# FFN of a two-layer encoder step: up projection as seven block products on sums of x halves, plain down products woven between

## The chip, the core and the metric

The kernel runs on one NeuronCore of a Trainium2 chip. Five engines work at once, each through its own list of instructions in order, and wait for one another through semaphores: PE (TensorE, matrix products), DVE (VectorE), ACT (ScalarE), POOL (GpSimd) and SP, which here only issues DMAs. The metric is the device time of one execution in microseconds (us); lower is better.

## What is computed

Two layers, each on 576 tokens (64 of running streams, 512 of new ones). A layer is a mixer (GLA and RWKV-7 groups between an input and an output projection), and a convolutional feed-forward network (FFN), each added to `x`. Only the FFN is touched:

```python
def _conv_ffn(h, conv_prev, w_up, conv_w, conv_b, w_down):   # h = RMSNorm(x), D = 1024, F = 2816
    uv = jnp.einsum('bld,df->blf', h, w_up)                  # 1024 -> 2 * 2816
    u, gate = uv[..., :D_FF], uv[..., D_FF:]
    u_ext = jnp.concatenate([conv_prev.astype(u.dtype), u], axis=1)
    uc = conv_b + sum(conv_w[j] * u_ext[:, j:j + seq] for j in range(CONV_W))
    conv_new = u_ext[:, seq:]
    y = jnp.einsum('blf,fd->bld', jax.nn.gelu(uc, approximate=False) * gate, w_down)   # 2816 -> 1024
    return y, conv_new
```

## The kernel before

**Layout.** Activations lie transposed: 128 features on the partitions, the 576 tokens along the row, so `x` is eight tiles of 128 x 576. An output tile of a product is one row of blocks; it is made in two halves of 288 tokens (`HT`), each in a PSUM bank of its own.

**Precision.** Every fp32 product is made of three passes in the rounded type fp32r: weights and activations are split into a high part (`whi`, `xh`, `hh`, `Hhi`: a rounded copy, made by ACT) and a low part (`wlo`, `xl`, `hl`, `Hlo`: original less high part, made by POOL for the weights as loaded, and by DVE for activations and for sums of weights). The passes are high x high, high x low, low x high. So an output tile over `n` inner tiles costs PE 6n matmuls of 288 columns.

**Pairs.** Work runs in pairs of output tiles: slot 0 and slot 1 have their own raw weights (`raw`, 128 x 1024, one DMA of 512 KB), their `whi`/`wlo` and, in a plain pair, PSUM tensors `PS[0]` and `PS[1]`. For each slot: SP loads `raw` once POOL's last low part there is made (`load`, L453), ACT rounds (`split`, L1436), POOL subtracts (`split` of POOL, L635), PE multiplies (`dense`, L790), DVE reads PSUM.

**The FFN before** goes in three parts of 8, 8 and 6 inner tiles (`PARTS`). There are 22 up pairs, all plain: slot 0 gives `u`, slot 1 the gate of one inner tile, 2 x 8 x 6 = 96 matmuls. For each, DVE scales `u` by the norm (`nrs`) into `up` (L2669 to L2671), keeps the last two columns (L2675), does two of the three convolution taps (L2680, L2683; ACT the first, L1960), scales the gate (L2690), and after ACT's GELU (L1967) multiplies (L2693, L2695); ACT and DVE then make high and low parts of the inner tile. In the first two parts DVE also forms four sums of halves of inner tiles (`T1` to `T4`). The down products of these two parts (4 pairs each) are *folded*: a 2 x 2 block product made of seven block products instead of eight (Strassen-Winograd form). Its weights are four quarters `A11, A12, A21, A22`; DVE makes the sums `S1` to `S4` (L2603, 128 x 512 each) and their low parts (L2608), ACT the high parts (L1910), POOL the low parts of `A11, A12, A22` (L731). A folded pair is 7 x 4 x 3 = 84 matmuls (L1335 to L1337). It uses four banks, and the pairs take the two sets of four banks in turn (`quad_banks`). The third part's four down pairs are plain with 6 inner tiles. At a part's border one up pair is issued ahead of the folded pairs, so that its DVE work lies beside them.

**Order.** It is written out by hand for each engine. PE waits in `product` for the low part of its quarter (`d_rest`, `w_lo`, `d_lo`), for ACT's copies between banks (`d_copy`), and before the last product for a DVE add (`d_add`).

## Time and profile before

| | us |
|---|---|
| median of 3 runs (1603.68 to 1604.71) | 1604.25 |
| the profiled execution: its time | 1609.08 |
| the profiled execution: its span | 1607.1 |
| PE busy, DVE busy, ACT busy, POOL busy in it | 1571.3, 1101.5, 707.8, 601.8 |

The profile is of one execution; it is read by engine, by stretch and by single rows. Busy time of DVE and POOL holds also the time in which an instruction has begun and is held up, so that a long row is not always long work. The FFN of layer 0 runs from about 390 to 808 us, that of layer 1 from about 1180 to 1594 us.

### The profile page before, as it was taken

The page shows a single profiled execution, that of the slowest core. Times are in us where ns is not written, and L with a number is a line of the kernel's source. Part 1 is how long each engine was busy: PE and PEld are TensorE (multiplying, and loading weights), DVE is VectorE, ACT ScalarE, POOL GpSimd, SP SyncE. Part 2 cuts the span into 40 slices and gives each one's busy share as a digit, 9 for nine tenths or more (in the row PEclk, how much of TensorE's full clock was granted, in tenths as well). Part 3 has the DMA queues.
Part 4 walks back from the last instruction along what each step waited for, and adds up shares of the span by engine and source line. Part 5 has one row for each costly group of instructions (what it writes and reads, how often), then busy time and mean ns, then how long its engine had stood idle before and what let it go on. Part 6 is the DMA issues. An engine that isn't in the chain of part 4 may idle for free.

```text
span 1607.1 us, 40959 instructions
## 1 busy us (share of the span) xinstructions
PE 1571.3 (98%) x17831; PEld 1530.0 (95%) x17831; DVE 1101.5 (69%) x1747; ACT 707.8 (44%) x1174; POOL 601.8 (37%) x394
## 2 busy tenths in 40 slices
PE   8999999999999999999999999999999999999997
PEld 7999989899999999999999999888999999999997
DVE  4679656675778677856647894566667786787664
ACT  5545356553334333433454644556433343334334
POOL 5345422223344343434333453122234434343331
PEclk9999999999999999999999999999999999999999
DMA  5222210012322322232332222000223232323222
GB/s 157 66 80 79 66 43 4 4 35 83 88 80 73 99 80 88 83 94 74 89 96 74 72 79 74 10 4 4 60 80 90 81 92 80 92 66 105 83 73 90
DMA packets 219123, 115.42 MB, mean 72 GB/s; under 512 B 9588, under 2 KB 216706, under 8 KB 218946
## 3 DMA queue, kind: packets, MB, share of 16 engines
q1 hardware_dynamic: 218866, 112.79, 24.7%
q8 instruction: 141, 2.31, 0.6%
q14 instruction: 36, 0.29, 0.1%
q10 hardware_dynamic: 80, 0.02, 0.0%
HBM read 109.27 MB, written 3.53 MB: 70 GB/s over the span
## 4 chain that ended last, share of the span: by engine, by line
PE 89%; DVE 5%; issue 2%; DMA 2%; POOL 1%; ACT 1%; SPq 0%; DVEq 0%; ACTq 0%
PE ps L758 31%; PE ps L759 31%; PE ps L1335 3%; PE ps L1337 3%; PE ps L1336 3%; PE ps L1008 2%; PE ps L1011 2%; PE ps L1005 2%; DMA raw<-in_ffn_w_down 1%; DVE Tall L2603 1%; PE ps L970 1%; POOL wlo L731 1%; PE ps L982 1%; PE ps L1073 1%; PE ps L763 1%
## 5 line engine op out<-in xcount | busy, mean ns | idle before, releaser
L635 POOL TENSOR_TENSOR wlo<-raw,whi 128x1024 fp32r<-128x1024 f32 (+1 forms) x169 | 432.3, 2558 | 621.2 <-ACT whi L1436 621.2
L1436 ACT ACTIVATE whi<-raw 128x1024 fp32r<-128x1024 f32 (+1 forms) x170 | 176.6, 1039 | 384.1 <-PE ps L759 359.4
L758 PE MATMUL ps<-xh,whi 128*128 128x288 f32 x1120 | 331.7, 296 | 1.8 <-DVE xl L2017 1.8
L759 PE MATMUL ps<-xh,whi 128*128 128x288 f32 x1120 | 329.4, 294 | 0.0
L758 PE MATMUL ps<-xl,whi 128*128 128x288 f32 x1120 | 329.3, 294 | 0.0
L759 PE MATMUL ps<-xl,whi 128*128 128x288 f32 x1120 | 329.3, 294 | 0.0
L758 PE MATMUL ps<-xh,wlo 128*128 128x288 f32 x1120 | 329.1, 294 | 0.0
L759 PE MATMUL ps<-xh,wlo 128*128 128x288 f32 x1120 | 328.8, 294 | 0.0
L758 PEld LDWEIGHTS ps<-xh,whi 128*128 128x128 f32 x1120 | 210.2, 188 | 3.8 <-issue 3.1
L759 PEld LDWEIGHTS ps<-xh,whi 128*128 128x128 f32 x1120 | 210.2, 188 | 0.2
L759 PEld LDWEIGHTS ps<-xl,whi 128*128 128x128 f32 x1120 | 210.2, 188 | 0.0
L759 PEld LDWEIGHTS ps<-xh,wlo 128*128 128x128 f32 x1120 | 210.0, 188 | 0.0
L758 PEld LDWEIGHTS ps<-xl,whi 128*128 128x128 f32 x1120 | 210.0, 188 | 0.0
L758 PEld LDWEIGHTS ps<-xh,wlo 128*128 128x128 f32 x1120 | 210.0, 188 | 0.0
L731 POOL TENSOR_TENSOR wlo<-raw,whi 128x512 fp32r<-128x512 f32 x48 | 69.6, 1460 | 120.7 <-ACT whi L1910 120.7
L2680 DVE SCALAR_TENSOR_TENSOR cv<-up,par,cv 128x578 f32<-128x578 f32 x44 | 70.9, 1611 | 27.3 <-ACT cv L1960 27.3
L1335 PE MATMUL ps<-Hhi,whi 128*128 128x288 f32 x256 | 76.0, 297 | 6.1 <-DVE wlo L2608 6.1
L1008 PE MATMUL ps<-work 64*64 64x64 f32 x1152 | 79.3, 218 | 1.8 <-issue 1.7
L1967 ACT ACTIVATE gl<-cv 128x578 f32<-128x578 f32 x44 | 30.4, 690 | 110.6 <-DVE cv L2683 110.6
L1011 PE MATMUL ps<-work 64*64 64x64 f32 x1152 | 74.3, 219 | 3.1 <-issue 3.0
L1337 PE MATMUL ps<-Hhi,wlo 128*128 128x288 f32 x256 | 75.3, 294 | 0.0
L1336 PE MATMUL ps<-Hlo,whi 128*128 128x288 f32 x256 | 75.2, 294 | 0.0
(370 smaller groups left out, 3628.9 us busy)
## 6 DMA issues: line engine op xcount, KB each, us to landing
raw<-in_ffn_w_up SPq DMA_DIRECT2D x88, 512.0 KB, 3.8
raw<-in_w_in SPq DMA_DIRECT2D x52, 512.0 KB, 3.8
raw<-in_ffn_w_down SPq DMA_DIRECT2D x32, 512.0 KB, 4.0
raw<-in_w_out SPq DMA_DIRECT2D x16, 512.0 KB, 4.1
raw<-in_ffn_w_down SPq DMA_DIRECT2D x16, 384.0 KB, 3.4
xin<-in_x_prompt SPq DMA_DIRECT2D x4, 512.0 KB, 7.1
out<-xin SPq DMA_DIRECT2D x8, 256.0 KB, 2.9
out<-RW SPq DMA_DIRECT2D x16, 64.0 KB, 2.2
```

Of the source, the lines that this page charges most:

```text
L635: e.tensor_tensor(wlo[s][:, 0:width], raw[s][:, 0:width], whi[s][:, 0:width].bitcast(F32), ALU.subtract).then_inc(w_lo[s], 1)
L731: lo = e.tensor_tensor(by_tile(D_lo[name]), A[name], by_tile(D_hi[name]).bitcast(F32), ALU.subtract)
L758: e.matmul(acc(out)[:, 0], lhsT, rhs[:, 0:HT], start=start, stop=stop)
L759: return e.matmul(acc(out)[:, 1], lhsT, rhs[:, HT:TOK], start=start, stop=stop)
L1005: mm = e.matmul(powers[h, X, 0], d[h, hp, X, 2], d[h, hp, X, 0], start=True, stop=True)
L1008: mm = e.matmul(powers[h, X, 1], d[h, hp, X, 0], d[h, hp, X, 2], start=True, stop=True)
L1011: mm = e.matmul(product[h, X], d[h, hp, X, 2], d[h, hp, X, 1], start=True, stop=True)
L1335: e.matmul(out, wh, Hhi[:, col, j], start=fresh and j == 0, stop=False, skip_group_check=True)
L1336: e.matmul(out, wh, Hlo[:, col, j], start=False, stop=False, skip_group_check=True)
L1337: mm = e.matmul(out, wl, Hhi[:, col, j], start=False, stop=j == FH - 1, skip_group_check=True)
L1436: e.activation(whi[s][:, 0:width], raw[s][:, 0:width], ACT.Copy).then_inc(w_hi[s], 1)
L2680: e.scalar_tensor_tensor(out=cv[:, :], in0=up[:, 1:3 + TOK], scalar=par[:, cw + FF + f:cw + FF + f + 1], in1=cv[:, :], op0=ALU.mult, op1=A ...
```

## The change

- **Up**: of 22 up pairs in a layer the first stays plain. The other 21 are folded, with halves of tokens and even and odd tiles of `x` as blocks. The four sums of `x` halves that this wants (`Xhi`, `Xlo`) are made once a layer, during the output projection of the mixer: for each pair of `x` tiles ACT writes two scaled copies (`xpair`) and rounds the four sums, DVE makes the sums (`mix_tokens`) and their low parts (`mix_lo`).
- So the weight sums, low parts and high parts that were made for 8 folded down pairs in a layer are now made for 21 up pairs. All 21 use the same four banks (0 to 3). The results are read by `folded_up` of DVE, which adds the `v` part that ACT moves out of its bank (`move_v`).
- **Down**: parts of 2, 4, 4, 4, 4 and 4 inner tiles. The down pairs are all plain. Those of the first five parts (20 in a layer, `mixed_products`) are woven between the up pairs from the third on, one after each, with banks 4 to 7 and 24 or 48 matmuls each; their weights have their own raw tiles (`draw`) and loads. The last part's four pairs (48 matmuls each) end the layer as before.

The constants:

```diff
-PARTS = (8, 8, 6)
-FOLDED = len(PARTS) - 1
-F_AT = (0, 8, 16)
-FH = PARTS[0] // 2
+PARTS = (2, 4, 4, 4, 4, 4)
+F_AT = (0, 2, 6, 10, 14, 18)
+MIXED = len(PARTS) - 1
+FH = KT // 2
```

SP (down loads and up loads in turn) and POOL (low parts of weights):

```diff
+                for f in range(1, FF):
+                    if f >= 2:
+                        load_down(*mixed_down(f))
+                    if f + 1 < FF:
+                        load_up(f + 1)
...
+                for f in range(0, FF):
+                    if f + 1 < FF:
+                        quad_rest(f + 1, "A11")
+                    if f >= 2:
+                        down_rest(*mixed_down(f), 1)
+                        down_rest(*mixed_down(f), 0)
+                    if f + 1 < FF:
+                        quad_rest(f + 1, "A12")
+                        quad_rest(f + 1, "A22")
```

PE:

```diff
+                def folded_up(f):
+
+                    m = folded(l, f)
+                    if f == 1:
+                        pe.wait_ge(xm_lo, (l + 1) * FH)
+                    pe.wait_ge(psum_free[0], turn(0, l, PAIRS["ffn"] + f))
+                    product(f, "P1", bank_a, True)
+                    product(f, "P5", bank_v, True)
+                    pe.wait_ge(d_copy, nth(AC_C, m, "b"))
+                    product(f, "P6", bank_b, False)
+                    product(f, "P2", bank_a, False)
+                    pe.wait_ge(d_copy, nth(AC_C, m, "c"))
+                    product(f, "P7", bank_b, False)
+                    product(f, "P3", bank_c, False)
+                    pe.wait_ge(u_add, nth(DV_U, m, "c22"))
+                    product(f, "P4", bank_b, False)
...
+                def mixed_products(g, it):
+
+                    q, n = down(l, g, it), PARTS[g]
+                    hi, lo = hh[:, slots(g)], hl[:, slots(g)]
+                    for s in range(2):
+                        pe.wait_ge(e_lo[s], q + 1)
+                        pe.wait_ge(e_free[s], q)
+                        for kt in range(n):
+                            if it == 0 and s == 0:
+                                pe.wait_ge(f_dve, (l * FF + F_AT[g] + kt + 1) * len(F_DV))
+                            wh, wl = (down_weights(w, s, n, kt) for w in (whi_all, wlo_all))
+                            for lhsT, rhs, first, last in ((wh, hi[:, kt], kt == 0, False), (wh, lo[:, kt], False, False),
+                                                           (wl, hi[:, kt], False, kt == n - 1)):
+                                mm = both(PS[2 + s], lhsT, rhs, first, last)
+                        mm.then_inc(e_done[s], 1)
+
+                for s in range(2):
+                    dense(s, turn(s, l, PAIRS["ffn"]), xh, xl, KT, n_lo if s == 0 else None, (l * NORMS + 1) * KT)
+                    if s == 0:
+                        pe.wait_ge(kept, l * 4 + 4)
+                        norm_sum(l * NORMS + 1)
+                for f in range(1, FF):
+                    folded_up(f)
+                    if f == 2:
                         pe.wait_ge(n_rs, 2 * (l * NORMS + 1) + 2)
+                    if f >= 2:
+                        mixed_products(*mixed_down(f))
```

ACT:

```diff
+                for f in range(1, FF):
+                    more = f + 1 < FF
+                    copy_b(f)
+                    if more:
+                        quad_hi(f + 1, "A11")
+                    else:
+                        split(0, turn(0, l, PAIRS["ffn"] + FF), DW)
+                    if f >= 2:
+                        down_hi(*mixed_down(f), 1)
+                    move_v(f)
+                    if f >= 2:
+                        down_hi(*mixed_down(f), 0)
+                    copy_c(f)
+                    if more:
+                        for name in ("S2", "A12", "S3", "S4"):
+                            quad_hi(f + 1, name)
+                    else:
+                        ac.wait_ge(d_prod, nth(PE_D, folded(l, f), "P2"))
+                        split(1, turn(1, l, PAIRS["ffn"] + FF), DW)
+                    conv_first(f)
+                    if more:
+                        quad_hi(f + 1, "A22")
+                    gelu(f)
+                    if more:
+                        quad_hi(f + 1, "S1")
+                    inner_hi(f)
```

DVE:

```diff
+                def mix_tokens(it):
+
+                    n = (l * FH + it) * 4
+                    dv.wait_ge(xp_done, 2 * (l * FH + it) + 2)
+                    dv.wait_ge(xm_lo, l * FH + it)
+                    even, odd = ([xpair[:, i, b * HT:(b + 1) * HT] for b in range(2)] for i in range(2))
+                    e.tensor_tensor(xmix[:, T1], even[0], even[1], ALU.subtract).then_inc(xm_done, 1)
+                    e.tensor_tensor(xmix[:, T3], odd[1], even[1], ALU.subtract).then_inc(xm_done, 1)
+                    dv.wait_ge(xm_done, n + 1)
+                    e.scalar_tensor_tensor(out=xmix[:, T2], in0=odd[1], scalar=-1.0, in1=xmix[:, T1],
+                                           op0=ALU.mult, op1=ALU.subtract).then_inc(xm_done, 1)
+                    dv.wait_ge(xm_done, n + 3)
+                    e.scalar_tensor_tensor(out=xmix[:, T4], in0=xmix[:, T2], scalar=-1.0, in1=odd[0],
+                                           op0=ALU.mult, op1=ALU.subtract).then_inc(xm_done, 1)
...
+                def folded_up(f):
+
+                    m, more = folded(l, f), f + 1 < FF
+                    own = [turn(s, l, PAIRS["ffn"] + f) + 1 for s in range(2)]
+                    if f >= 3:
+                        add_down(*mixed_down(f - 1), 1)
+                    if more:
+                        for name in SUMS:
+                            quad_sum(f + 1, name)
+                    pad(f)
+                    dv.wait_ge(d_prod, nth(PE_D, m, "P2"))
+                    e.tensor_tensor(up[:, 2:2 + DEC], bank_a[:, 0:DEC], nrs[:, 0:DEC], ALU.mult)
+                    e.tensor_tensor(up[:, 4 + DEC:4 + HT], bank_a[:, DEC:HT], nrs[:, DEC:HT], ALU.mult).then_inc(u_add, 1)
+                    if more:
+                        quad_lo(f + 1, "S2")
+                    dv.wait_ge(d_copy, nth(AC_C, m, "v"))
+                    dv.wait_ge(d_prod, nth(PE_D, m, "P7"))
+                    e.tensor_tensor(hf[:, HT:TOK], bank_b, vs[:, :], ALU.add).then_inc(u_add, 1)
+                    added_up(f, "c22")
+                    e.tensor_tensor(hf[:, HT:TOK], hf[:, HT:TOK], nrs[:, HT:TOK], ALU.mult).then_inc(u_add, 1)
+                    dv.wait_ge(d_prod, nth(PE_D, m, "P3"))
+                    e.tensor_tensor(up[:, 4 + HT:4 + TOK], bank_c, vs[:, :], ALU.add).then_inc(psum_free[0], 1)
+                    dv.wait_ge(psum_free[0], own[0])
+                    e.tensor_tensor(up[:, 4 + HT:4 + TOK], up[:, 4 + HT:4 + TOK], nrs[:, HT:TOK], ALU.mult).then_inc(u_add, 1)
+                    added_up(f, "u12")
+                    keep_last(f)
+                    if more:
+                        quad_lo(f + 1, "S3")
+                    dv.wait_ge(tile_done[1], own[1])
+                    e.tensor_tensor(hf[:, 0:HT], bank_b, nrs[:, 0:HT], ALU.mult).then_inc(psum_free[1], 1)
+                    if more:
+                        quad_lo(f + 1, "S4")
+                    conv_rest(f)
+                    if f >= 2:
+                        add_down(*mixed_down(f), 0)
+                    if more:
+                        quad_lo(f + 1, "S1")
+                    gated(f, -1.0)
+                    inner_lo(f)
```

**DVE, one period of the FFN.** A row is one instruction: line, operation, output and inputs, size, and the semaphores that it waits for. Before, in an up pair of an even inner tile (from the row that fills the convolution's left edge to the one that gives the low part):

```order
L2659 COPY up<-par 128x2 [waits f_dve]
L2669 TENSOR_TENSOR up<-ps,nrs 128x64 [waits tile_done0]
L2670 TENSOR_TENSOR up<-ps,nrs 128x224
L2671 TENSOR_TENSOR up<-ps,nrs 128x288
L2675 COPY last_conv<-up 128x2 [waits psum_free0]
...
L2680 SCALAR_TENSOR_TENSOR cv<-up,par,cv 128x578 [waits f_cv]
L2683 SCALAR_TENSOR_TENSOR cv<-up,par,cv 128x578 [waits f_dve]
L2690 TENSOR_TENSOR h_first<-ps,nrs 128x576 [waits tile_done1]
L2693 SCALAR_TENSOR_TENSOR h_first<-gl,h_first 128x64 [waits f_gelu,psum_free1]
L2695 SCALAR_TENSOR_TENSOR h_first<-gl,h_first 128x512
L2699 TENSOR_TENSOR h_first<-h_first 128x288 [waits f_dve]
L2644 TENSOR_TENSOR Hlo<-h_first,Hhi 128x2x288 [waits f_hi]
```

Now, the first half of a period with an up pair and a woven down pair (`Tall` holds the sums `S1` to `S4` of the next pair's weights, `x` is the residual stream):

```order
L2809 TENSOR_TENSOR x<-x,ps 128x576 [waits e_done1]
L2691 TENSOR_TENSOR Tall<-raw 128x512 [waits d_lo,w_loaded0,w_loaded1]
L2691 TENSOR_TENSOR Tall<-raw,Tall 128x512 [waits d_sum,d_lo]
L2691 TENSOR_TENSOR Tall<-raw 128x512 [waits d_lo]
L2691 TENSOR_TENSOR Tall<-raw,Tall 128x512 [waits d_sum,d_lo]
L2705 COPY up<-par 128x2 [waits f_dve]
L2776 TENSOR_TENSOR up<-ps,nrs 128x64 [waits d_prod]
L2777 TENSOR_TENSOR up<-ps,nrs 128x224
L2696 TENSOR_TENSOR slo<-Tall,shi 128x512 [waits d_hi]
L2782 TENSOR_TENSOR hf<-ps,vs 128x288 [waits d_prod,d_copy]
L2784 TENSOR_TENSOR hf<-hf,nrs 128x288 [waits u_add]
L2786 TENSOR_TENSOR up<-ps,vs 128x288 [waits d_prod]
```

The second half, up to the next period's first row:

```order
L2788 TENSOR_TENSOR up<-up,nrs 128x288 [waits psum_free0]
L2712 COPY last_conv<-up 128x2 [waits u_add]
...
L2696 TENSOR_TENSOR slo<-Tall,shi 128x512 [waits d_hi]
L2794 TENSOR_TENSOR hf<-ps,nrs 128x288 [waits tile_done1]
L2696 TENSOR_TENSOR slo<-Tall,shi 128x512 [waits d_hi]
L2718 SCALAR_TENSOR_TENSOR cv<-up,par,cv 128x578 [waits f_cv]
L2721 SCALAR_TENSOR_TENSOR cv<-up,par,cv 128x578 [waits f_dve]
L2809 TENSOR_TENSOR x<-x,ps 128x576 [waits e_done0]
L2696 TENSOR_TENSOR wlo<-Tall,whi 128x512 [waits d_hi]
L2729 SCALAR_TENSOR_TENSOR hf<-gl,hf 128x64 [waits f_gelu,psum_free1]
L2731 SCALAR_TENSOR_TENSOR hf<-gl,hf 128x512
L2738 SCALAR_TENSOR_TENSOR hl<-hf,hh 128x576 [waits f_hi]
```

Four sums, four low parts and two adds into `x` have come into every period; a period has 25 DVE instructions where an up pair had 13 or 15.

**POOL, at the end of a part.** Before, the three quarters of a folded pair and then the two slots of the next plain pair:

```order
L731 TENSOR_TENSOR wlo<-raw,whi 128x512 [waits d_hi]
L731 TENSOR_TENSOR wlo<-raw,whi 128x512 [waits w_hi0]
L731 TENSOR_TENSOR wlo<-raw,whi 128x512 [waits w_hi1]
L635 TENSOR_TENSOR wlo<-raw,whi 128x1024 [waits w_hi0]
L635 TENSOR_TENSOR wlo<-raw,whi 128x1024 [waits w_hi1]
```

Now, in every period from the third up pair on (`Ei` holds the down weights as loaded):

```order
L755 TENSOR_TENSOR wlo<-raw,whi 128x512 [waits d_hi]
L765 TENSOR_TENSOR wlo<-Ei,whi 128x2x256 [waits e_hi1]
L765 TENSOR_TENSOR wlo<-Ei,whi 128x512 [waits e_hi0]
L755 TENSOR_TENSOR wlo<-raw,whi 128x512 [waits w_hi0]
L755 TENSOR_TENSOR wlo<-raw,whi 128x512 [waits w_hi1]
```

The two instructions of 1024 elements in an up pair have become three of 512, and two of 512 for the down pair stand between the first and the second of them.

## Rows read from the trace of the kernel before

**Rows 1.** The page: busy time and share by engine, granted clock in 40 slices.
```profile
PE 1571.3 (98%) x17831; PEld 1530.0 (95%) x17831; DVE 1101.5 (69%) x1747; ACT 707.8 (44%) x1174; POOL 601.8 (37%) x394
...
PEclk9999999999999999999999999999999999999999
```

**Rows 2.** A stretch: us; busy PE, PEld, DVE, ACT, POOL; clock, DMA share, GB/s.
```profile
476.00:727.00 251.00, 247.18 (x1855) 246.49 (x1854) 186.19 (x284) 94.94 (x134) 98.23 (x49) 0.99 0.30 86
```

**Rows 3.** Waits of PE in 345:810: us in total, times, longest.
```profile
PE ps L1335 <- DVE wlo L2608: 3.8, 2, 2.4
```

**Rows 4.** Timeline of PE: start, duration, instruction; in a plain and a folded pair.
```profile
559.81 0.29 PE L758 MATMUL ps<-xl,whi 128*128 128x288 f32 x1
...
560.87 0.29 PE L758 MATMUL ps<-xh,wlo 128*128 128x288 f32 x1
...
505.13 0.29 PE L1335 MATMUL ps<-Hhi,whi 128*128 128x288 f32 x1
...
505.92 0.29 PE L1335 MATMUL ps<-Hhi,whi 128*128 128x288 f32 x1
```

**Rows 5.** Lines of DVE: duration in ns, least/median/most, first and last start.
```profile
L2603 DVE TENSOR_TENSOR Tall<-raw x16: 678/684/1042, 501.6 to 689.6; 128x512 f32<-128x512 f32 x16
...
L2608 DVE TENSOR_TENSOR slo<-Tall,shi x24: 677/686/1784, 505.8 to 694.3; 128x512 fp32r<-128x512 f32 x24
...
L2571 DVE TENSOR_TENSOR x<-x,ps x24: 750/754/756, 770.6 to 1593.4; 128x576 f32<-128x576 f32 x24
...
L2683 DVE SCALAR_TENSOR_TENSOR cv<-up,par,cv x12: 821/822/1740, 480.0 to 712.6; 128x578 f32<-128x578 f32 x12
...
L2659 DVE COPY up<-par x37: 155/170/2249, 485.9 to 1544.8; 128x2 f32<-128x2 f32 x37
```

**Rows 6.** The line of POOL in folded pairs, the same way.
```profile
L731 POOL TENSOR_TENSOR wlo<-raw,whi x24: 1280/1296/2209, 499.4 to 692.6; 128x512 fp32r<-128x512 f32 x24
```

**Rows 7.** Timeline of POOL; in brackets the idle time before and what ended it.
```profile
657.28 3.57 POOL L731 TENSOR_TENSOR wlo<-raw,whi 128x512 fp32r<-128x512 f32 x2 [4.98 <-ACT whi L1910]
663.93 2.55 POOL L731 TENSOR_TENSOR wlo<-raw,whi 128x512 fp32r<-128x512 f32 x2 [3.08 <-ACT whi L1910]
```

**Rows 8.** Timeline of DVE in 652 to 667.
```profile
652.24 0.68 DVE L2603 TENSOR_TENSOR Tall<-raw 128x512 f32<-128x512 f32 x1
653.02 0.69 DVE L2603 TENSOR_TENSOR Tall<-raw,Tall 128x512 f32<-128x512 f32 x1
653.63 0.69 DVE L2603 TENSOR_TENSOR Tall<-raw 128x512 f32<-128x512 f32 x1
...
657.10 0.82 DVE L2680 SCALAR_TENSOR_TENSOR cv<-up,par,cv 128x578 f32<-128x578 f32 x1
657.96 1.74 DVE L2683 SCALAR_TENSOR_TENSOR cv<-up,par,cv 128x578 f32<-128x578 f32 x1
659.61 2.38 DVE L2608 TENSOR_TENSOR slo<-Tall,shi 128x512 fp32r<-128x512 f32 x2
...
664.17 0.45 DVE L2622 TENSOR_TENSOR x<-x,ps 128x288 f32<-128x288 f32 x1
...
665.99 1.04 DVE L2603 TENSOR_TENSOR Tall<-raw 128x512 f32<-128x512 f32 x1 [1.00 <-DMA raw<-in_ffn_w_down]
```

**Rows 9.** Timeline of ACT in folded pairs, and DVE waiting for ACT's high part.
```profile
659.73 0.69 ACT L1967 ACTIVATE gl<-cv 128x578 f32<-128x578 f32 x1 [1.72 <-DVE cv L2683]
...
675.11 0.63 ACT L1910 ACTIVATE whi<-raw 128x512 fp32r<-128x512 f32 x1 [0.65 <-PE ps L1337]
...
583.71 2.06 DVE L2644 TENSOR_TENSOR Hlo<-h_first,Hhi 128x576 fp32r<-128x576 f32 x1 [0.81 <-ACT Hhi L1942]
```

**Rows 10.** Timeline of DVE in the last plain down pairs of layer 0.
```profile
772.32 1.70 DVE L2017 SCALAR_TENSOR_TENSOR xl<-x,gains,xh 128x576 fp32r<-128x576 f32 x1 [0.93 <-ACT xh L1446]
```

**Rows 11.** The last stretch, columns as in rows 2.
```profile
1590.00:1607.00 17.00, 8.96 (x60) 8.02 (x58) 4.89 (x7) 6.31 (x10) 0.00 (x0) 0.81 0.41 139
```

**Rows 12.** The page: a weight DMA: count, size and median us from issue to landing.
```profile
raw<-in_ffn_w_up SPq DMA_DIRECT2D x88, 512.0 KB, 3.8
```

More of the change, by code:

```diff
@@ new lines, in _ @@
+                load_up(0)
+                load_up(1)
+                for f in range(1, FF):
[3 more added lines that the diff above has]
+                        load_up(f + 1)
+                sp.wait_ge(d_sum, nth(SUMS, folded(l, FF - 1), "S4"))
+                for it in range(KT // 2):
+                    for s in range(2):
+                        load(s, turn(s, l, PAIRS["ffn"] + FF + it),
+                             raw[s][:, 0:DW].rearrange("p (k m) -> p k m", m=P), down_rows(MIXED, it, s))
@@ L1457, in spare_split, with mix_hi, added @@
                 e.activation(spare_hi[:, :], raw[0][:, 0:KT * P], ACT.Copy).then_inc(w_hi[0], 1)
-            def added(l, pair, c, width, after, rows=False, ready=False):
+            def mix_hi(l, it):
+                ac.wait_ge(xm_done, (l * FH + it + 1) * 4)
+                e.activation(Xhi[:, :, it], xmix[:, :, :], ACT.Copy).then_inc(xm_hi, 1)
+            def added(l, pair, c, width, after, rows=False, ready=False, mix=False):
                 for k in range(KT):
@@ L1478, in added @@
                         square(c, k)
+                    if mix and k >= 2 and s == 0:
+                        mix_hi(l, it - 1)
+                    if mix and s == 1:
+                        ac.wait_ge(xm_done, (l * FH + it) * 4)
+                        for i in range(2):
+                            e.activation(xpair[:, i], x[:, k - 1 + i, :], ACT.Copy, scale=gain(c, k - 1 + i)).then_inc(xp_done, 1)
                     if rows and k == 2:
@@ new lines, in quad_hi @@
+                def quad_hi(f, name):
+                    k = [turn(s, l, PAIRS["ffn"] + f - 1) + 1 for s in range(2)]
+                    if f == 1 and name in ("A11", "S1"):
+                        ac.wait_ge(tile_done[0], k[0])
+                    elif f == 1 and name in ("A12", "A22"):
+                        ac.wait_ge(tile_done[1], k[1])
+                    elif f == 1:
+                        ac.wait_ge(xm_lo, (l + 1) * FH)
+                    elif name == "S1" and f > 2:
+                        ac.wait_ge(e_done[0], down(l, *mixed_down(f - 1)) + 1)
+                    elif name == "S1":
+                        ac.wait_ge(tile_done[0], k[0])
+                    elif name == "A22":
+                        ac.wait_ge(tile_done[1], k[1])
+                    else:
+                        reader = dict(A11="P1", A12="P2", S2="P6", S3="P7", S4="P3")[name]
+                        ac.wait_ge(d_prod, nth(PE_D, folded(l, f - 1), reader))
@@ new lines, in copy_c @@
+                def copy_c(f):
+                    ac.wait_ge(d_prod, nth(PE_D, folded(l, f), "P6"))
+                    ac.wait_ge(psum_free[0], turn(0, l, PAIRS["ffn"] + f))
+                    e.activation(bank_c, bank_b, ACT.Copy).then_inc(d_copy, 1)
+                quad_hi(1, "A11")
+                for name in ("S2", "S3", "S4"):
+                    quad_hi(1, name)
+                conv_first(0)
+                quad_hi(1, "A12")
+                quad_hi(1, "A22")
+                gelu(0)
@@ new lines, in inner_lo, with plain_up @@
+                def inner_lo(f):
+                    slot = f if f < PARTS[0] else (f + 2) % (2 * max(PARTS))
+                    dv.wait_ge(f_hi, l * FF + f + 1)
+                    e.scalar_tensor_tensor(out=hl[:, slot, :], in0=hf[:, :], scalar=1.0, in1=hh[:, slot, :].bitcast(F32),
+                                           op0=ALU.mult, op1=ALU.subtract).then_inc(f_dve, 1)
+                def plain_up():
+                    t0, t1 = (turn(s, l, PAIRS["ffn"]) + 1 for s in range(2))
+                    pad(0)
@@ L2739, in _, with add_down @@
+                def add_down(g, it, s):
+                    xt = x[:, 2 * it + s, :]
+                    dv.wait_ge(e_done[s], down(l, g, it) + 1)
+                    e.tensor_tensor(by_half(xt), by_half(xt), acc(PS[2 + s]), ALU.add).then_inc(e_free[s], 1)
+                plain_up()
+                for f in range(1, FF):
+                    folded_up(f)
+                add_down(*mixed_down(FF - 1), 1)
+                add_tiles(PAIRS["ffn"] + FF, (l + 1) * NORMS)
             dv.wait_ge(y_rs, 2)
```

536 lines of the change are left out of this document (196 added, 340 removed).

## The prediction

> **What bounds the kernel now.** I read the page first: PE is busy 98% of the span at the full granted clock, DVE 69%, POOL 37% [rows 1]. Then the waits of PE: from 345 to 810 us, a whole FFN with the end of the stage before it, PE waits 3.8 us, twice, for DVE at the start of folded pairs [rows 3]. So PE sets the pace everywhere in the FFN. Its price is the distance of starts, not the length of a row: 8 matmuls from 559.81 to 560.87 in a plain pair and 6 from 505.13 to 505.92 in a folded one, 0.132 us each in both [rows 4]. Time can be won only by fewer matmuls, and it is won only as long as DVE, ACT and POOL keep up. In the stretch with one folded part DVE is already busy 186 of 251 us [rows 2]. That is the engine to cost.
>
> **What is removed.** Matmuls of one layer before: 22 x 96 + 8 x 84 + 4 (L1355) + 4 x 72 = 3076. After: 96 + 21 x 84 for up, and for down 22 inner tiles x 8 output tiles x 6 = 1056, together 2916. That is 160 fewer in a layer, 320 in all, by 0.132 = **42.2 us** less work of PE. The 3.8 us of waits in a layer go with the old folded pairs: I take 7.6 for both layers.
>
> **What is added on DVE.** From the third up pair on, a period is one folded up pair and one woven down pair. PE needs (84 + 48) x 0.132 = 17.4 us for it with 4 inner tiles, (84 + 24) x 0.132 = 14.3 us in the four periods of the part with 2. The new order gives DVE 25 instructions in it. By duration [rows 5]: four sums of 0.69 and four low parts of 0.69, 5.5; two adds into `x` of 0.75, 1.5; two taps of 0.82, 1.6; the product with the GELU, 0.69 and about 0.2 for its 64 columns, 0.9; low part of the inner tile, 0.8 as the tap of nearly the same size; five instructions of 288 columns at 0.45 (L2622 [rows 8]), 2.25; the first 64 and 224 columns of `up`, 0.6 (estimate between 0.17 and 0.45 each); three small copies of 0.17, 0.5. Sum 13.7. Neighbours overlap by 0.08 (the third sum starts 0.61 after the second, which lasts 0.69), but one that needs its own engine's last result starts 0.1 after its end [rows 8]; five do. Some 17 overlaps less five such steps leave **12.5 us** of work.
>
> **What holds DVE up.** DVE and POOL do not run side by side when both read two tiles of SBUF. POOL has two instructions from 657.28 to 660.85 [rows 7], and DVE's rows of that time are in [rows 8]. A tap of 0.82 that starts at 657.96 in it lasts 1.74, held by 0.92; the next two low parts take 2.38 instead of 1.30, held by 1.08; and POOL's pair takes 3.57 instead of 2.55. They alternate. The add at 664.17, which has one operand in PSUM, runs within POOL's next pair at its plain 0.45. A copy of two elements, 0.17 by itself, has lasted 2.25 [rows 5]. So each POOL instruction of 512 elements that meets such work of DVE costs DVE about 1.0 us (POOL's own row is 1.30 [rows 6]; the sum at 665.99 shows that DVE is let go some 0.14 before that row ends).
>
> The Trainium skill says more than that ("SBUF — State Buffer", section "SBUF: two separate sides"): the port pair that VectorE and GpSimd share is an exclusive lock held for the full instruction. By the full 1.30 of POOL's row a hold would cost 1.3; the rows show 0.92 and 1.08, so the trace bears out the lock and not its full length.
>
> Now place the five. POOL's four for `A11`, the two down slots and `A12` are released by ACT one after another as P1 to P2 end. DVE is just then in its four sums, all of SBUF only, one of POOL's between each and the next. The fifth, `A22`, is released when P4 ends, and meets the first tap. All five meet SBUF-only work: 5 x 1.0 = 5.0 us (bounds: 2.5, if half fall beside PSUM reads or idle time, and 6.5).
>
> DVE also waits for ACT twice in a period. After the second tap ACT has a GELU (0.69) and the high part of `S1` (0.63) to do, and DVE only an add of 0.75: 0.7 idle. Then the high part of the inner tile: 0.8 idle, as 0.81 now [rows 9]. Together 1.5.
>
> **The sum by period.** DVE: 12.5 + 5.0 + 1.5 = 19.0 us against PE's 17.4. Nothing gives this back: the four banks are the same each time, and P4 waits for the add of P7's bank (`c22`), which stands behind the four sums in DVE's list. So PE loses 1.6 us before P4 in each of 16 periods: 25.6 a layer, and about 2.2 once more when the part with 2 tiles ends. In the three later periods of that part, two holds are of half size: 12.5 + 3 x 1.0 + 2 x 0.5 + 1.5 - 0.7 (less waiting, since DVE is further behind) = 17.3 against 14.3, 3.0 each, 9.0.
>
> **The head of a layer.** P5 of the first folded pair needs the low part of `S1`, and its high part stands behind ACT's GELU of the plain pair. When the plain pair ends, DVE has before it the rest of a tap (about 1), a held second tap (1.8), a held low part (1.7), two more (1.2), the gate's scaling (0.7) and this low part with its start (0.9), to which ACT's handovers add about 1.7. That is 9.0, and P1 covers 1.6: PE stands **7.4**. The second folded pair follows with no down pair between: scaling 0.45, low part 0.7, held tap 1.8, tap 0.8, GELU 0.7, high part 0.6, low part 0.7, handovers 0.5 = 6.2 against 1.6, and 1.2 more before its P4: **5.8**.
>
> **The end of a layer.** The last four down pairs give PE 24 x 0.132 = 3.2 us an output tile, not 4.8. DVE's chain there is add 0.75, idle 0.93 for ACT, low part 0.82 to 1.70 [rows 10], square about 0.7: 3.2 to 4.1. With two banks in turn and POOL's shorter instructions I take its lower end, 0.5 a layer; the upper is 7.
>
> **The sums of x** lie in the mixer's output projection. A pair there lasts 96 x 0.132 = 12.7 us; DVE has about 2 x 3.3 and gets 4 x 0.45 and one of 1152 columns (about 1.3), ACT four more rows. Cover is there; nothing. **Loads** of 512 KB land 3.8 us after issue [rows 12], and a period asks for 1.5 MB in 19 us; the up load waits for the sums and for POOL, some 8 us ahead of use. Nothing, or 1 us a period if late.
>
> **Total.** Waits a layer: 25.6 + 2.2 + 9.0 + 7.4 + 5.8 + 0.5 = 50.5. Both layers: -42.2 - 7.6 + 101.0 = **+51 us**. Against the profiled execution's 1609.1 that is 1660; the median of the runs is 4.8 lower, so **1655 us**.
>
> **Rivals.**
> 1. PE keeps the pace. If the holds fall beside PSUM reads and idle time and cost half (2.5), DVE's period is 16.5, below 17.4. Only heads (about 11 a layer) and the 2-tile part (1.5) stay: -42.2 - 7.6 + 2 x 13 = -24, **1580 us**. For it: before, long stretches have the same kind of DVE work with no wait of PE [rows 3]. Against: there POOL has two instructions a pair, now five in the span of the sums.
> 2. In between. The point of balance is a hold total of about 3.6 a period: then 0.2 x 16, 1.9 x 3 and about 13 for heads and entry, 22 to 25 a layer, and the gain is used up. 3.6 to 4.5 gives **1600 to 1630**.
> 3. Longer holds. If a hold is as long as POOL's row, 1.30 [rows 6], a period is 20.4 and PE waits 3.0: +1.4 x 16 and +1.2 x 3 in each layer, **1707 us**. The two holds above speak against it. This is what the Trainium skill's rule on the shared pair ("SBUF — State Buffer", same section) would give. Shorter of the same kind: handovers of 0.1 throughout, and the layer's end at its upper bound, add some 12 each, **1680**.
> 4. PE's clock. In the last stretch, with PE busy half the time, the granted clock is 0.81 [rows 11], so a part of it ran at the lower of the two levels, 1.2 GHz. The waits of 7.4 and 5.8 could bring that for a few us after each: 4 x 2 = +8, **1663**, inside the forecast's range.
>
> **How the numbers follow.** Forecast with rival 4, 1630 to 1680: 0.64. Rival 1: 0.10. Rival 2: 0.15, a third of it within or below today's time. Rival 3: holds of the full row 0.04, slow handovers and the layer's end, above 1680, 0.04. That the weave stalls elsewhere (late down loads, ACT's copies between banks): 0.03, about 1690. A measurement of this kernel can tell 0.2%, some 3 us. Faster by more 0.13, within 0.02, slower 0.85. The range is 1608 to 1680: it leaves out rival 1, the lower part of rival 2 and what is above 1680, about 2 in 10.
>
> **What would show it.** Right: PE's waits in the FFN grow from 3.8 to about 50 us a layer, most of them in front of P4 (L1369), with DVE's add (L2782) as releaser, at a period of about 19 us; the sums (L2691) have a median near 1.7 instead of 0.69; at the head P5 waits 6 to 9 us for a low part. The matmul count falls by 320 in this list. Wrong: periods of 17.4 us and sums near 0.7 (rival 1); PE waiting for POOL or for copies (L2002, L2014); a released time that is DMA's.

## The result, and the profile after

| | before | after |
|---|---|---|
| median of the runs beside each other, us | 1604.48 (1603.68 to 1605.42) | 1659.22 (1657.79 to 1661.72) |
| span of the profiled execution, us | 1607.1 | 1658.4 |
| matmuls | 17831 | 17511 |

The changed kernel is slower: its time is 1.034 times that of before, 95% interval 1.0325 to 1.0361. Less work of TensorE gave a longer run.

The page of after, its line of busy time and, under it, the shares of the chain that ended last (before, 89% of that chain was PE and 5% DVE):

```profile
PE 1548.7 (93%) x17511; PEld 1497.0 (90%) x17511; DVE 1280.6 (77%) x2041; ACT 805.1 (49%) x1470; POOL 620.7 (37%) x468
...
PE 53%; DVE 33%; issue 9%; ACT 4%; DMA 1%; SPq 0%; DVEq 0%; ACTq 0%
```

Against [rows 1], PE has 22.6 us less of busy time (its modelled ends hide part of the 42), DVE 179 us more. POOL's total is nearly what it was, and this is what misleads: it has 74 instructions more, of other sizes. A third of the chain is now DVE's.

The waits of PE from 345 to 865 us, the FFN of layer 0 (columns as in [rows 3]):

```profile
PE ps L1369 <- DVE hf L2782: 23.3, 18, 2.4
PE ps L1369 <- DVE wlo L2696: 16.2, 6, 7.4
```

The first row is the wait before P4 for the add of P7's bank, 18 times: 14 of about 1.22 in the steady periods, and four in the part with two inner tiles and at its end. The second is the wait before P5 for the low part of `S1`, six times, two of them long. Where [rows 3] had 3.8 us there are now 39.5. The true loss is larger, since a matmul's modelled end lies some 0.16 us behind the start of what could follow.

One steady period on DVE (start and duration in us, instruction):

```profile
653.55 0.69 DVE L2691 TENSOR_TENSOR Tall<-raw 128x512 f32<-128x512 f32 x1
654.34 1.60 DVE L2691 TENSOR_TENSOR Tall<-raw,Tall 128x512 f32<-128x512 f32 x1
655.86 1.79 DVE L2691 TENSOR_TENSOR Tall<-raw 128x512 f32<-128x512 f32 x1
657.58 1.78 DVE L2691 TENSOR_TENSOR Tall<-raw,Tall 128x512 f32<-128x512 f32 x1
659.28 1.26 DVE L2705 COPY up<-par 128x2 f32<-128x2 f32 x1
...
661.49 0.44 DVE L2782 TENSOR_TENSOR hf<-ps,vs 128x288 f32<-128x288 f32 x1
...
665.03 1.85 DVE L2718 SCALAR_TENSOR_TENSOR cv<-up,par,cv 128x578 f32<-128x578 f32 x1
...
669.01 0.69 DVE L2696 TENSOR_TENSOR wlo<-Tall,whi 128x512 fp32r<-128x512 f32 x1 [0.61 <-ACT whi L1956]
...
671.19 0.76 DVE L2738 SCALAR_TENSOR_TENSOR hl<-hf,hh 128x576 fp32r<-128x576 f32 x1 [0.75 <-ACT hh L1996]
...
672.53 0.69 DVE L2691 TENSOR_TENSOR Tall<-raw 128x512 f32<-128x512 f32 x1
```

And POOL beside it:

```profile
653.82 1.57 POOL L755 TENSOR_TENSOR wlo<-raw,whi 128x512 fp32r<-128x512 f32 x1 [6.55 <-ACT whi L1956]
655.35 3.46 POOL L765 TENSOR_TENSOR wlo<-Ei,whi 128x512 fp32r<-128x512 f32 x2
658.77 1.75 POOL L755 TENSOR_TENSOR wlo<-raw,whi 128x512 fp32r<-128x512 f32 x1
664.87 1.39 POOL L755 TENSOR_TENSOR wlo<-raw,whi 128x512 fp32r<-128x512 f32 x1 [4.35 <-ACT whi L1956]
```

Read the two together. The first sum begins 0.27 before POOL does and takes its plain 0.69. The second, third and fourth each have a POOL instruction between themselves and the sum before; they last 0.91, 1.10 and 1.09 longer. The copy of two elements, 0.16 by itself, meets POOL's fourth and lasts 1.26. The first tap meets the fifth: 1.03 longer. Five POOL instructions, five holds, 5.2 us. The add that P4 waits for (661.49) stands behind four of them. The period is 18.98 (653.55 to 672.53).

PE at the same place: the last matmul of P3 and the first of P4, with what it waited for:

```profile
660.47 0.29 PE L1371 MATMUL ps<-xh,slo 128*128 128x288 f32 x1
...
661.99 0.40 PE L1369 MATMUL ps<-Xhi,whi 128*128 128x288 f32 x1 [1.23 <-DVE hf L2782]
```

From start to start 1.52, where 0.13 is the pitch: 1.39 lost. There are 14 such periods in each layer, all of 1.37 to 1.39.

The head of the layer, in stretches of 4 us (columns as in [rows 2]; the clock is the last but two):

```profile
404.00:408.00 4.00, 0.75 (x6) 0.51 (x4) 2.59 (x3) 3.69 (x6) 2.07 (x2) 1.00 0.00 0
408.00:412.00 4.00, 0.00 (x0) 0.00 (x0) 4.00 (x5) 1.17 (x2) 1.06 (x1) 0.66 0.69 199
412.00:416.00 4.00, 3.87 (x16) 3.87 (x17) 3.15 (x6) 1.94 (x4) 1.54 (x1) 0.50 0.43 129
416.00:420.00 4.00, 4.00 (x32) 4.00 (x31) 2.92 (x7) 1.57 (x3) 0.38 (x2) 0.99 0.02 4
...
428.00:432.00 4.00, 2.43 (x10) 2.43 (x11) 2.43 (x5) 2.50 (x6) 0.11 (x1) 0.72 0.31 94
432.00:436.00 4.00, 4.00 (x28) 4.00 (x28) 3.90 (x4) 1.77 (x5) 3.80 (x3) 0.85 0.00 0
```

PE starts nothing from 404.45 to 412.13. When it starts again it is granted 0.50, its lower level of 1.2 GHz, for about 4 us: its matmuls start every 0.24 us and not every 0.13, so that the stretch from 412 holds 16 of them and the next one 32. After the second wait (425 to 430) the same happens for some 3.5 us.

### The profile page after: what moved, and what is told of

It reads as the page before. It is cut to its first block, busy times and chain, and to the rows that moved or that the text cites. A ratio compares the mean times of both kernels' runs of the same rounds, so it can differ in the third digit from the quotient of the medians.

```text
span 1658.4 us, 41494 instructions
## 1 busy us (share of the span) xinstructions
PE 1548.7 (93%) x17511; PEld 1497.0 (90%) x17511; DVE 1280.6 (77%) x2041; ACT 805.1 (49%) x1470; POOL 620.7 (37%) x468
## 4 chain that ended last, share of the span: by engine, by line
PE 53%; DVE 33%; issue 9%; ACT 4%; DMA 1%; SPq 0%; DVEq 0%; ACTq 0%
PE ps L790 14%; PE ps L791 14%; DVE Tall L2691 8%; DVE slo L2696 4%; DVE cv L2718 4%; DVE up L2705 3%; DVE cv L2721 2%; PE ps L1043 2%; PE ps L1040 2%; PE ps L1369 2%; PE ps L1370 2%; PE ps L1371 2%; DVE x L2809 2%; PE ps L1037 1%; ACT whi L1956 1%
## 5 line engine op out<-in xcount | busy, mean ns | idle before, releaser
L755 POOL TENSOR_TENSOR wlo<-raw,whi 128x512 fp32r<-128x512 f32 x126 | 192.7, 1530 | 458.9 <-ACT whi L1956 458.9
L660 POOL TENSOR_TENSOR wlo<-raw,whi 128x1024 fp32r<-128x1024 f32 (+1 forms) x85 | 203.3, 2392 | 303.9 <-ACT whi L1474 303.9
L790 PE MATMUL ps<-xh,whi 128*128 128x288 f32 x448 | 134.2, 300 | 2.4 <-DVE xl L2081 1.8
L765 POOL TENSOR_TENSOR wlo<-Ei,whi 128x512 fp32r<-128x512 f32 (+1 forms) x80 | 127.8, 1616 | 14.2 <-ACT whi L1971 14.2
L790 PE MATMUL ps<-xh,wlo 128*128 128x288 f32 x448 | 131.9, 294 | 0.0
L791 PE MATMUL ps<-xh,wlo 128*128 128x288 f32 x448 | 131.7, 294 | 0.0
L791 PE MATMUL ps<-xh,whi 128*128 128x288 f32 x448 | 131.7, 294 | 0.0
L790 PE MATMUL ps<-xl,whi 128*128 128x288 f32 x448 | 131.6, 294 | 0.0
L791 PE MATMUL ps<-xl,whi 128*128 128x288 f32 x448 | 131.5, 293 | 0.0
L2691 DVE TENSOR_TENSOR Tall<-raw,Tall 128x512 f32<-128x512 f32 x84 | 123.7, 1473 | 4.7 <-DVE Tall L2691 0.5
L791 PE MATMUL ps<-hh,wlo 128*128 128x288 f32 x352 | 103.6, 294 | 0.0
L790 PE MATMUL ps<-hl,whi 128*128 128x288 f32 x352 | 103.6, 294 | 0.0
L790 PE MATMUL ps<-hh,whi 128*128 128x288 f32 x352 | 103.6, 294 | 0.0
L791 PE MATMUL ps<-hh,whi 128*128 128x288 f32 x352 | 103.5, 294 | 0.0
L791 PE MATMUL ps<-hl,whi 128*128 128x288 f32 x352 | 103.4, 294 | 0.0
L790 PE MATMUL ps<-hh,wlo 128*128 128x288 f32 x352 | 103.3, 293 | 0.0
```

What stands on the lines that cost most here:

```text
L660: e.tensor_tensor(wlo[s][:, 0:width], raw[s][:, 0:width], whi[s][:, 0:width].bitcast(F32), ALU.subtract).then_inc(w_lo[s], 1)
L755: lo = e.tensor_tensor(by_tile(D_lo[name]), A[name], by_tile(D_hi[name]).bitcast(F32), ALU.subtract)
L765: e.tensor_tensor(down_parts(wlo_all, s, n), down_raw(s, n), down_parts(whi_all, s, n).bitcast(F32), ALU.subtract).then_inc(e_lo[s], 1)
L790: e.matmul(acc(out)[:, 0], lhsT, rhs[:, 0:HT], start=start, stop=stop)
L791: return e.matmul(acc(out)[:, 1], lhsT, rhs[:, HT:TOK], start=start, stop=stop)
L2691: e.tensor_tensor(out, *terms, ALU.add).then_inc(d_sum, 1)
```

## The experiments

All ratios are to the kernel before, run beside each on the same chip; its medians there were 1602 to 1604.5 us. The first column is the number of the experiment below. "Sums" are the instructions of DVE that form S1 to S4.

| | kernel | median, us | ratio, 95% interval |
|---|---|---|---|
| | changed kernel | 1659.22 | 1.0343 [1.0325, 1.0361] |
| 1 | all five low parts on DVE | 1602.23 | 1.0002 [0.9993, 1.0011] |
| 2 | POOL's five at an eighth of the columns | 1586.41 | 0.9910 [0.9895, 0.9925] |
| 3 | the adds into x narrow | 1638.61 | 1.0226 [1.0209, 1.0243] |
| 4 | POOL only writes | 1585.91 | 0.9913 [0.9893, 0.9933] |
| 5 | POOL writes three times | 1585.58 | 0.9888 [0.9851, 0.9925] |
| 6 | POOL reads one tile | 1590.54 | 0.9928 [0.9905, 0.9950] |
| 7 | two low parts on DVE | 1615.50 | 1.0089 [1.0075, 1.0103] |
| 8 | PE kept busy in the head | 1651.09 | 1.0308 [1.0294, 1.0322] |
| 9 | five on DVE, head reordered | 1588.05 | 0.9917 [0.9905, 0.9930] |

**1. All five low parts from POOL to DVE.** DVE gets five instructions more a period and POOL none:

```diff
-                        po.wait_ge(d_hi, nth(AC_D, folded(l, f), "A11"))
...
+                        dv.wait_ge(d_hi, nth(AC_D, folded(l, f), "A11"))
...
                     pad(f)
+                    if more:
+                        quad_rest(f + 1, "A11")
+                    if f >= 2:
+                        down_rest(*mixed_down(f), 1)
+                        down_rest(*mixed_down(f), 0)
...
```

> The five low parts of weights in a period (three quarters of the next up pair, two halves of the down pair) are made by DVE and no longer by POOL; all results are computed. Theory (POOL's instructions hold DVE's back): DVE gets five instructions of 0.61 us start to start (3.1) and loses five holds of about 1.0 (5.2), and two of the five fill gaps in which it waits for ACT, so its period falls from 19.0 to below PE's 17.4: no wait of PE in the periods with four inner tiles, about 1.6 us instead of 2.8 in those with two; about 1600 us, between 1592 and 1608. Rival (the number of DVE instructions sets the pace, POOL works beside it at no cost): a period of 19.0 + 3.1 = 22 us, 100 us more, 1755 us.

Measured: 1602.23 us, ratio 1.0002 to before, so 3.3% faster than the changed kernel, although DVE got more instructions. Of the sums, those that read an earlier sum (least, median, most in ns), here and in the changed kernel:

```profile
L2663 DVE TENSOR_TENSOR Tall<-raw,Tall x84: 681/688/694, 401.9 to 1528.6; 128x512 f32<-128x512 f32 x84
```
```profile
L2691 DVE TENSOR_TENSOR Tall<-raw,Tall x84: 677/1602/1799, 402.0 to 1587.2; 128x512 f32<-128x512 f32 x84
```

DVE's busy time fell, from 1280.6 to 1214.8 us, with 206 instructions more. In the steady periods PE waits for nothing. What is left, 27 us in both layers, stands in the heads and in the part with two inner tiles; most of it is this row:

```profile
PE ps L1341 <- DVE wlo L2687: 22.2, 12, 4.4
```

**2. POOL's five at an eighth of the columns.**

```diff
-                    lo = e.tensor_tensor(by_tile(D_lo[name]), A[name], by_tile(D_hi[name]).bitcast(F32), ALU.subtract)
+                    lo = e.tensor_tensor(by_tile(D_lo[name])[:, :, 0:16], A[name][:, :, 0:16],
+                                         by_tile(D_hi[name])[:, :, 0:16].bitcast(F32), ALU.subtract)
...
```

> POOL's five instructions in a period cover 64 of their 512 columns (or 32 of 256), so most of the low parts of the FFN's weights are left as they were; everything else as in the changed kernel. Theory: holds shrink to a sixth, DVE's period is about 14.5, PE's 17.4 decides; 1.4 us of wait in each of 15 periods and most of 2.8 in the others go, the head's shrink by about 3: about 1589 us, between 1580 and 1598. Rival (DVE's own work sets the pace): no change, 1659. Rival (PE's waits come from ACT's copies or from loads): no change, 1659.

Measured: 1586.41 us. The order of everything, the semaphores and DVE's own list are those of the changed kernel; only the length of POOL's rows differs, and by the ratios some 70 us are gone. This is the price of the holds and of what follows from them, all told. (POOL's low parts are also ready sooner here; experiment 5, where POOL is busy with each for as long as before and the time is the same, shows that this is not what was won.)

**3. The adds into x narrow.**

```diff
-                    e.tensor_tensor(by_half(xt), by_half(xt), acc(PS[2 + s]), ALU.add).then_inc(e_free[s], 1)
+                    e.tensor_tensor(by_half(xt)[:, :, 0:8], by_half(xt)[:, :, 0:8], acc(PS[2 + s])[:, :, 0:8], ALU.add).then_inc(e_free[s], 1)
```

> The two adds of the woven down pair into the residual cover 16 of their 576 columns, so most of the down result of the first five parts is left out. That takes 2 x 0.58 us of work from DVE, work that does not meet POOL. Theory (DVE's list is the bound, but its first add stands in front of a wait for ACT's high part, so that only the second counts): 0.6 us a period in 16 to 20 periods of two layers, about 1640 us. Rival (all work of DVE counts alike): 1.2 us a period, 1613 us. Rival (DVE is not the bound): 1659.

Measured: 1638.61 us. The adds went from 0.75 to 0.17 each, 1.2 us less work of DVE in a period, and the loss before P4 fell from 1.39 to 0.64 in a steady one. So DVE sets the period, and only a part of the 1.2 is won, 0.75 where the theory had 0.6: the work saved by the first add came back as idle time before the low part of `S1`, 1.20 instead of 0.61. This tells a DVE that is short of time from a wait for POOL itself, which less work of DVE should not have shortened.

**4. POOL writes and does not read.** A memset of the same columns takes the place of each subtraction:

```diff
-                    lo = e.tensor_tensor(by_tile(D_lo[name]), A[name], by_tile(D_hi[name]).bitcast(F32), ALU.subtract)
+                    lo = e.memset(by_tile(D_lo[name]).bitcast(F32), 0.0)
...
```

> POOL writes zeros over the same columns instead of the difference, five times a period: it reads nothing, and the low parts of the FFN's weights are zero. Tells apart what holds DVE. Theory A (it is POOL's reading of SBUF that holds a DVE instruction with two inputs in SBUF): the sums fall to their plain 0.69 and the time to that of the narrow run, about 1589 us. Theory B (any POOL instruction holds it, by its length): holds by the length of the zero writes, which no run shows yet; with 0.5 us each about 1625, with 1.2 us each 1659.

Measured: 1585.91 us, the sums at their plain 0.69. But a memset takes 0.53 and not 1.3, so this alone left open whether it was only too short to be noticed.

**5. POOL writes three times.** The same, each memset three times over:

```diff
+                    for _ in range(2):
+                        e.memset(out, 0.0).then_inc(zeroed, 1)
+                        z[0] += 1
+                        po.wait_ge(zeroed, z[0])
+                    return e.memset(out, 0.0)
...
```

> As the kernel in which POOL only writes zeros, but each of the five writes them three times, one after another, so that POOL is busy with a low part for 3 x 0.53 = 1.6 us, longer than with the subtraction (1.3 to 1.5). Low parts are zero. Theory (writes of POOL don't hold DVE, however long): sums 0.69, copy 0.16, about 1586 us. Rival (the single write was too short, 0.53 us, to be seen; time in which POOL uses SBUF is what holds): sums of 1.2 to 1.7 and 1620 to 1660 us.

Measured: 1585.58 us. POOL in the span of the sums, and the last three sums and the copy:

```profile
644.98 1.11 POOL L753 MEMSET wlo<- 128x512 f32 x2 [6.30 <-ACT whi L1964]
646.15 0.53 POOL L756 MEMSET wlo<- 128x512 f32 x1
```
```profile
644.42 0.69 DVE L2699 TENSOR_TENSOR Tall<-raw,Tall 128x512 f32<-128x512 f32 x1
645.03 0.69 DVE L2699 TENSOR_TENSOR Tall<-raw 128x512 f32<-128x512 f32 x1
645.63 0.69 DVE L2699 TENSOR_TENSOR Tall<-raw,Tall 128x512 f32<-128x512 f32 x1
646.24 0.46 DVE L2713 COPY up<-par 128x2 f32<-128x2 f32 x1
```

The sums run straight through POOL's memsets. Its time in SBUF is not what holds them; what it reads is. One row goes against what was expected: the copy of two elements lasts 0.46 (the median of 44) instead of 0.16 and ends as POOL's memset ends (646.70 and 646.68), so a copy of DVE's is held by a write as well.

**6. POOL reads one tile and not two.** A copy of the raw columns in place of the subtraction:

```diff
-                    lo = e.tensor_tensor(by_tile(D_lo[name]), A[name], by_tile(D_hi[name]).bitcast(F32), ALU.subtract)
+                    lo = e.tensor_copy(by_tile(D_lo[name]), A[name])
...
```

> The five instructions of POOL copy raw columns to the low part of the same size: they read one tile of SBUF and not two, so the low parts are wrong by their meaning (the high part isn't subtracted). POOL's copy of 512 elements takes 0.68 us elsewhere in this trace, the subtraction 1.28. Theory A (only an instruction of POOL that reads two tiles holds DVE): the four sums in a steady period take 0.69 each, the copy into up 0.16, about 1586 us. Theory B (one read is enough): sums beside a POOL row take longer by up to its 0.68, about 1.2 each; DVE's period is then 14.0 + 5 x 0.5 = 16.5, still under TensorE's 17.4, so the time is about 1590 and only the rows of DVE tell the two apart.

Measured: 1590.54 us, and the rows decide for theory B:

```profile
647.96 1.10 DVE L2690 TENSOR_TENSOR Tall<-raw 128x512 f32<-128x512 f32 x1
648.98 1.09 DVE L2690 TENSOR_TENSOR Tall<-raw,Tall 128x512 f32<-128x512 f32 x1
650.00 0.57 DVE L2704 COPY up<-par 128x2 f32<-128x2 f32 x1
```
```profile
647.56 0.96 POOL L755 CAST wlo<-raw 128x512 fp32r<-128x512 f32 x1 [7.27 <-ACT whi L1955]
648.47 2.08 POOL L765 CAST wlo<-Ei 128x512 fp32r<-128x512 f32 x2
```

(CAST is POOL's copy, with the conversion of type.) One read holds too, for 0.41 each: the POOL instruction is shorter (0.73 at its least in this stretch) and so is the hold. Four of DVE's rows are held in a period, two sums and the copy by 0.41 each and the first tap by 0.35, together 1.6 and not 5.2. That is under the balance, and PE keeps the pace.

**7. Two of the five to DVE**, the low parts of the down tiles; POOL keeps the three of the up pair.

```diff
                     pad(f)
+                    if f >= 2:
+                        down_rest(*mixed_down(f), 1)
+                        down_rest(*mixed_down(f), 0)
```

> Only the two low parts of the down tiles move from POOL to DVE; POOL keeps the three of the up pair. All is computed. Theory (each reading POOL row costs DVE about 1.05 us of hold, done by DVE itself it costs 0.61): 2 x (1.05 - 0.61) = 0.9 us less a period in the 16 steady ones, 2 x (1.05 - 0.35) = 1.4 less in the three with two inner tiles, so 2 x (16 x 0.9 + 3 x 1.4) = -37: about 1622 us, between the changed kernel (1659) and the one with all five moved (1602). The waits before P4 fall from about 1.4 to about 0.5 us each. Rival (the hold is not per POOL row, DVE is simply short of time): two more rows of 0.61 a period make it slower, 1659 + 2 x 16 x 1.2 = 1698 us.

Measured: 1615.50 us, the right side and 6 us under the expected 1622. A steady period is 17.6 us (the copies into `up` stand at 645.36 and 662.96), and PE hardly waits in it: balance is reached with three reading rows of POOL left. Two rows show why the expected time was too high:

```profile
644.15 0.68 DVE L2681 TENSOR_TENSOR Tall<-raw 128x512 f32<-128x512 f32 x1
...
647.06 1.40 DVE L2693 TENSOR_TENSOR slo<-Tall,shi 128x512 fp32r<-128x512 f32 x1
```

The third sum is plain again, with no POOL row near. And POOL's row for `A12` (646.63 to 647.92) now lies half beside reads of PSUM, and the hold that is left of it is 0.71, not 1.1. The three holds are 0.91, 0.71 and 1.03, 2.65 in all where 3 x 1.05 was expected. Where the POOL instruction falls is a part of its price.

**8. PE kept busy in the head.** Matmuls into a bank that nothing reads fill the two long waits:

```diff
                     product(f, "P1", bank_a, True)
+                    for n in range({1: 52, 2: 28}.get(f, 0)):
+                        e.matmul(bank(7)[:, 0:HT], Xhi[:, T1, 0, 0:P], xh[:, 0, 0:HT], start=True, stop=True,
+                                 skip_group_check=True)
                     product(f, "P5", bank_v, True)
```

> The changed kernel, with 52 matmuls of 128x288 (6.9 us) into an unused bank in the wait before P5 of pair 1 and 28 (3.7 us) in that of pair 2; their result is read by nobody and all else is computed. They fit into the waits of 7.5 and 4.4 us. Theory (the granted clock falls because TensorE stands still there, and the fall costs about 3.5 us a layer): the clock stays near 1.00 through both waits and the time falls to 1652 us; less, down to 1656, where DVE is late anyway. Rival (the fall of the clock costs nothing, since DVE sets the pace of that stretch): 1659 us with the clock at 1.00. Rival (the clock falls for another reason): it falls as before, and 1659.

Measured: ratio 1.0308 against 1.0343 for the changed kernel, 5.6 us less, with 160 matmuls more. The stretch that had 0.50 has now 1.00 and 31 matmuls instead of 16:

```profile
412.00:416.00 4.00, 4.00 (x31) 4.00 (x31) 3.90 (x8) 2.23 (x5) 1.65 (x2) 1.00 0.01 2
```

So in the changed kernel the clock falls because PE stands still, and its fall has a price: 5.6 us of the expected 7. The two intervals together leave some 4 us of doubt in that number; the granted clock leaves none about its sense.

**9. A kernel that beats both.** On top of experiment 1, S1 of pair 1 is split second and not last, `A12` and `A22` earlier, and in all periods S1's parts go ahead of GELU and of the add into `x`:

```diff
-                for name in ("S2", "S3", "S4"):
-                    quad_hi(1, name)
-                conv_first(0)
+                quad_hi(1, "S2")
+                quad_hi(1, "S1")
                 quad_hi(1, "A12")
+                conv_first(0)
...
-                    gelu(f)
                     if more:
                         quad_hi(f + 1, "S1")
+                    gelu(f)
...
-                    if f >= 2:
-                        add_down(*mixed_down(f), 0)
                     if more:
                         quad_rest(f + 1, "A22")
+                    if more:
                         quad_lo(f + 1, "S1")
+                    if f >= 2:
+                        add_down(*mixed_down(f), 0)
```

> On top of the kernel with all five low parts on DVE (1602 us): for pair 1 S1 is split second and not last, A12 and A22 earlier so that pair 2 loads earlier, and in every period S1 is split before GELU and its low part taken before the add into x. All is computed. Theory (what is left over the bound of TensorE are waits of 4.5 and 4.1 us before P5 of pairs 1 and 2 and 0.85 in the next four, all for a low part of S1 that comes last in its queue): 4.8 us a layer less and a part of the clock's loss, 1590 us, 0.7% below the kernel before (1602 here). Rival (the head is bound by the loads and by DVE's work as a whole; the waits only move): 1600 us.

Measured: 1588.05 us, ratio 0.9917. It computes everything, with the 320 matmuls less that the change wanted, and is 0.8% faster than before and 4.1% faster than the changed kernel. The waits of PE on the folded line, both layers, by releaser:

```profile
PE ps L1355 <- DVE wlo L2704: 4.7, 2, 3.1
PE ps L1355 <- ACT ps L1988: 4.4, 8, 0.6
PE ps L1355 <- DVE hf L2799: 3.9, 6, 2.1
PE ps L1355 <- ACT ps L2000: 3.5, 2, 1.7
PE ps L1355 <- DVE wlo L2688: 1.7, 2, 0.9
```

That is 18.2 us, where experiment 1 had 27. These 9 us are less than the 14 that were won. The granted clock can be a part of the rest: from 412 to 416 us it is 1.00 here and 0.50 in experiment 1, though it falls later in this head too (0.76 and 0.81 from 416 to 424). How the rest divides is not shown.

## Why the prediction was right, step by step

The predicted time was 1655 us; 1659.2 came out. The mechanism that carried it, POOL's instructions holding DVE beyond PE's pace, stands by experiments 1 to 6. That the time came so close is in part luck: several terms were off, in both directions. The steps:

- **PE's work, -42.2 us.** The matmuls are 320 fewer as counted. Where nothing holds PE (experiment 4), a period of 132 takes 17.51 (the copies into `up` from 540.80 to 663.40, seven periods), 17.4 was taken.
- **The old waits, -7.6.** They were 3.8 in layer 0 but only 2.3 in layer 1; from start to start both together lose 6.7.
- **DVE's period, 12.5 + 5.0 + 1.5 = 19.0.** Measured 18.98: holds 5.2, waits for ACT 0.61 and 0.75, and 12.4 of its own. Each term came within 0.2. The holds fell a little otherwise than told: the first sum is free, and the copy after the sums takes the fourth POOL instruction. The 12.5 was luck: its own figures (13.7, less 17 x 0.08, plus 5 x 0.1) give 12.8. That would have made the period 19.3 and the time some 10 us more (16 periods of 0.3 in each layer).
- **The steady loss, 16 x 1.6 = 25.6 a layer, and 2.2 at the entry.** Of the 16 periods the first is the entry: it was put at 1.6 + 2.2 = 3.8 and costs 3.9 (1.33 before P5, 2.56 before P4). The last folded pair has no sums for a next one in front of it and loses nothing. The other 14 take 19.0 against 17.51: 20.9.
- **Three periods with two inner tiles, 3.0 each.** Measured 2.75, but in two places: 1.3 before P5 and 1.45 before P4.
- **The head, 7.4 and 5.8.** From start to start PE loses 7.55 and 4.42. The first is right; in the second the low part of `S1` came as told (4.6), but the further 1.2 before its P4 did not.
- **The end of a layer, 0.5.** Measured 0.6 after layer 0; after layer 1 PE waits as long as before.
- **The clock (rival 4).** Not in the sum, put at 4 a layer. It happened: some 31 matmuls a layer start 0.24 apart instead of 0.13, about 3.5 us, and by experiment 8 it costs 2.8. It made up for most of what the second pair and the steady periods were short of.

The losses by steps are 20.9 + 3.9 + 8.2 + 7.6 + 4.4 + 3.5 = 48.5 a layer, and 0.6 after layer 0, where 50.5 a layer was forecast. With -42.2 and -6.7 this gives +48.7; the spans differ by 51.3. Some 2.6 us are not placed. One sum of the chances is off as well: what the range leaves out adds up to 0.26, not to 2 in 10.

**The rivals.** Rival 1 (holds cost half, 1580) failed by its premise, since every one of the five meets work that it holds; with the holds all but gone and the heads left, experiments 2, 4 and 5 gave 1586. Rival 2's balance, holds of 3.6 a period, fits: 5.2 loses 1.5 a period, and 1.6 in experiment 6 loses nothing. Experiment 7 stands nearly at the balance: holds of 2.65 and 1.2 more of DVE's own work, 3.85 together, and a period of 17.6 against 17.51. Rival 3, a hold as long as POOL's row, falls: 0.9 to 1.1 where POOL's row by itself is 1.28 to 1.39, and 0.41 where it is 0.73. The first tap shows where the difference lies: it starts 0.16 after POOL's row (665.03 and 664.87) and is let go, 1.03 late, at 666.06, 0.20 before that row ends (666.26). The Trainium skill ("SBUF — State Buffer", section "SBUF: two separate sides") has the pair of ports locked for the full instruction; the trace agrees with the lock, but DVE is let go some 0.2 us before POOL's row ends.

## What to carry to other kernels

An instruction moved from DVE to POOL is not free because POOL is idle: here each subtraction of 512 elements on POOL cost DVE 0.9 to 1.1 us, while DVE does it itself in 0.6 from start to start (experiment 7, two from 645.43 to 646.63), so the helping engine took more than it gave. Look whether the rows of one DVE line have two lengths (0.69 and 1.6 to 1.8 here); if they do, put the other engine's rows beside them before you count its capacity. And where a change saves work of the engine that bounds, add up the period of the next engine with its holds first: the 42 us saved here only count once DVE's period is under 17.5. Even then the heads of the layers decide: experiment 1, where PE waits nowhere in the steady periods, only came level with before (1602), and a better order in the heads brought the gain (experiment 9, 1588).
